# A depthwise convolution as block-Toeplitz matmuls: from 4 phases and 32 channels per block to 8 phases and 16 channels

## The reference, cut to what matters

```python
proj = h @ w_in                                   # (B, T, 5*D)
a, bg, u_pool, gate_a, gate_b = split(proj)
glu = a * sigmoid(bg)
conv, new_conv = causal_depthwise_conv(glu, conv_prev, conv_w, conv_b)   # width 31, per channel
y_a = silu(layer_norm(conv, conv_ln_g, conv_ln_b)) @ w_conv_out
pooled, new_pool = multiscale_pool(u_pool, pool_prev, pos0)  # trailing means over 2, 4, 8, 16
y_b = (einsum(pooled, pool_w) * pool_scale) @ w_pool_out
merged = sigmoid(gate_a) * y_a + sigmoid(gate_b) * y_b
return merged @ w_out, new_conv, new_pool
```

## Time and profile before

| | |
|---|---|
| median of 3 runs | 1577.0 us (1576.28 to 1577.05) |
| the profiled execution | 1571.29 us, span 1569.7 us (core 5, the slowest) |
| spans of the 8 cores | 1556.7 to 1569.7 us |
| busy, share of the span | PE 94%, PEld 55%, DVE 44%, ACT 30%, POOL 9% |
| mixer of A: GLU stage, pool and convolution stage | 545 to 605 us, 605 to 676 us |
| mixer of B: GLU stage, pool and convolution stage | 818 to 878 us, 878 to 946 us |

### The profile page before, as it was taken

The page is one execution under the profiler, slowest core; times in us unless marked ns, Lnnn a source line. Parts: engine busy times, 40 slices in busy tenths (PEclk is TensorE's granted clock), DMA queues, the critical chain, the costliest instruction groups (busy, mean ns, idle before and its releaser), DMA issues.

```text
span 1569.7 us, 24460 instructions; the slowest of 8 cores (1556.7 to 1569.7 us)
## 1 busy us (share of the span) xinstructions
PE 1479.4 (94%) x9258; PEld 856.3 (55%) x9258; DVE 688.6 (44%) x935; ACT 472.9 (30%) x688; POOL 133.9 (9%) x253
## 2 busy tenths in 40 slices
PE   0799999999899999999999999999999999999995
PEld 0466666544344457765664564445666665444454
DVE  1223323565222465972377687237431134441255
ACT  0011112253112264672127456113531111421124
POOL 2011111000110000000000000000000010000000
PEclk9999999999999999999999999999999999999998
DMA  9989999869977868635386964457586465584522
GB/s 185 180 141 196 196 215 186 167 110 190 186 137 145 144 155 232 182 72 131 55 174 143 243 182 105 97 104 154 118 178 131 74 132 97 111 170 84 113 70 99
DMA packets 94980, 227.03 MB, mean 145 GB/s; under 512 B 10848, under 2 KB 36192, under 8 KB 94688
## 3 DMA queue, kind: packets, MB, share of 16 engines
q0 software_dynamic: 37136, 124.11, 48.6%
q1 hardware_dynamic: 57728, 101.36, 20.9%
HBM read 299.64 MB, written 40.11 MB: 216 GB/s over the span
## 4 chain that ended last, share of the span: by engine, by line
PE 84%; DMA 9%; DVE 3%; ACT 2%; issue 2%; SPq 0%; DVEq 0%; ACTq 0%; POOL 0%; POOLq 0%
PE ps L354 78%; PE ps L769 4%; DMA VS<-pool_w 3%; DMA ring<-ffn_w_in 2%; DMA VS<-R 2%; DMA XS<-tp_dr 1%; DMA ring<-w_ada 1%; DVE VB L322 1%; PE ps L418 1%; DVE hA L319 1%; ACT L315 1%; ACT scr L315 0%; PE ps L544 0%; ACT rstd_sb L315 0%; ACT VB L315 0%
## 5 line engine op out<-in xcount | busy, mean ns | idle before, releaser
L354 PE MATMUL ps<-hA,ring 128*128 128x348 bf16 x3072 | 467.2, 312 | 8.1 <-DMA ring<-ffn_w_in 3.6
L354 PE MATMUL ps<-hB,ring 128*128 128x512 bf16 x2048 | 450.9, 380 | 10.0 <-DVE mpv L513 5.3
L354 PE MATMUL ps<-R,ring 128*128 128x348 bf16 (+3 forms) x2378 | 398.7, 327 | 0.0
L354 PEld LDWEIGHTS ps<-hA,ring 128*128 128x128 bf16 x3072 | 298.1, 97 | 170.1 <-issue 9.6
L354 PEld LDWEIGHTS ps<-hB,ring 128*128 128x128 bf16 x2048 | 200.0, 98 | 250.6 <-issue 15.7
L315 ACT ACTIVATE scr<-ps 128x1044 f32<-128x1044 f32 (+1 forms) x136 | 140.3, 1032 | 633.8 <-PE ps L354 629.8
L354 PEld LDWEIGHTS ps<-R,ring 128*128 128x128 bf16 x2378 | 229.3, 97 | 163.1 <-issue 0.2
L319 DVE TENSOR_TENSOR R<-ps,scr 128x1024 bf16<-128x1024 f32 (+2 forms) x112 | 128.8, 1156 | 429.9 <-PE ps L354 387.0
L315 ACT ACTIVATE scr<-VB 128x1044 f32<-128x1044 f32 (+3 forms) x56 | 51.5, 919 | 296.8 <-DVE VB L322 121.1
L322 DVE SCALAR_TENSOR_TENSOR VB<-ps,modT,XS 128x1024 f32<-128x1024 f32 (+4 forms) x56 | 55.1, 983 | 97.1 <-PE ps L354 94.1
L303 POOL DMA_DIRECT2D ring<-ffn_w_in x88 | 46.6, 531 | 470.8 <-PE ps L354 440.2
(11 more groups left out here) (121 smaller groups left out, 802.7 us busy)
## 6 DMA issues: line engine op xcount, KB each, us to landing
ring<-ffn_w_in POOLq DMA_DIRECT2D x88, 512.0 KB, 10.0
ring<-w_in POOLq DMA_DIRECT2D x40, 512.0 KB, 7.5
ring<-w_ada POOLq DMA_DIRECT2D x36, 512.0 KB, 15.8
ring<-ffn_w_out POOLq DMA_DIRECT2D x48, 352.0 KB, 6.3
XS<-tp_dr SPq DMA_DIRECT2D x48, 288.0 KB, 4.5
tp_dr<-VS SPq DMA_DIRECT2D x32, 288.0 KB, 15.5
XS<-x_b SPq DMA_DIRECT2D x16, 512.0 KB, 9.8
VS<-R SPq DMA_DIRECT2D x128, 64.0 KB, 5.6
```

The lines of the kernel that those rows point to most:

```text
L354: ins = e.matmul(o, lt, rt[:, c0:c0 + n], start=(i == 0), stop=(i == nk - 1))
```

## The change

It goes to NQ = 8 phases of NM = 128 columns: token 8m+q stands at phase q. A block now holds 16 channels by 8 phases, so 64 groups (NG) instead of 32, and ND = 5 shifts instead of 9. A group is 5 matmuls of 128 columns and has 160 KB of Toeplitz weights.

- Convolution: 640 matmuls of 128 columns for both mixers, instead of 576 of 256. A conv_unit still has 512 columns: 4 groups, each a recorded operation of its own with its own wait. 12 Toeplitz slots of 640 columns (nine in XS, three in poolw); two groups lie in one row of tp_dr.
- ACT: per unit 4 Identity of 128 columns and one Square of 512 that reads conv from SBUF, instead of 2 and 2 of 256 from PSUM. Silu: 4 of 128 per unit instead of 2 of 256.
- glu_move and the copies after Silu: 8 copies of 16 channels in runs of 128 bf16 (256 bytes) per chunk, instead of 4 with runs of 512 bytes.
- Pooling: halos of 4 columns instead of 6; the sum for windows of 8 is now two DVE instructions. In A the copies into U take several phases at once: 7 pieces instead of 6.
- conv_stats: 4 matmuls of 256 columns instead of 2 of 512; mean and rstd have 128 columns instead of 256.
- build_toep: 32 products of 1280 columns instead of 1152, in 6 slots instead of 7; cwv lies in hB and is 640 KB instead of 288 KB.

```diff
-NQ = 4
-NM = 256
-NG = 32
-ND = 9
-GHAL = 8
-UH = 6
+NQ = 8
+NM = 128
+NG = 64
+ND = 5
+GHAL = 4
+UH = 4
 UR = UH + NM
-NTOEP = 7
+NTOEP = 12
+TW = ND * 128
...
             def glu_move(c):
                 st = glst[:, c % 2, :]
-                pairs = [(GP[:, 4 * c + i, GHAL:], st[32 * i:32 * i + 32, :].rearrange("c (q m) -> c q m", q=NQ)) for i in range(4)]
+                n = 128 // NQ
+                pairs = [(GP[:, NQ * c + i, GHAL:], st[n * i:n * i + n, :].rearrange("c (q m) -> c q m", q=NQ)) for i in range(NQ)]
...
-                if c < NTOEP:
-                    tload(c)
+                for t in range(12 * c // 8, 12 * (c + 1) // 8):
+                    tload(t)
...
+            UG = 512 // NM
+
             def conv_unit(u):
                 bk = 6 + u % 2
-
-                def cmm(e):
-                    ins = None
-                    for t in range(2):
-                        gi = 2 * u + t
+                for t in range(UG):
+                    gi = UG * u + t
+
+                    def cmm(e, gi=gi, t=t):
+                        ins = None
                         for d in range(ND):
...
-                    act(sq[:, t * NM:(t + 1) * NM], ps[:, bk, t * NM:(t + 1) * NM], AF.Square, bias=cpv[:, 0, gi:gi + 1])
+                cu = lambda w: conv[:, UG * w:UG * w + UG, :].rearrange("p t n -> p (t n)")
+                act(sq, cu(u), AF.Square)
...
-                        tt(P[:, :, 4:UR], Q[:, :, 4:UR], Q[:, :, 3:UR - 1], ALU.add)
+                        wsum(P, Q, 3, 4)
...
-                            dma("sp", "sw%d" % (c % 4), [(d_[32 * i:32 * i + 32, :].rearrange("c (q m) -> c q m", q=NQ), s_[:, i, :]) for i in range(4)], [s_], [d_])
+                            dma("sp", "sw%d" % (c % 4), [(d_[nch * i:nch * i + nch, :].rearrange("c (q m) -> c q m", q=NQ), s_[:, i, :])
+                                                         for i in range(NQ)], [s_], [d_])
```

More of the change, by code:

```diff
@@ L843, in mixer @@
                     conv_unit(2 * i - 1)
-            conv_unit(NG // 2 - 2)
-            conv_unit(NG // 2 - 1)
+            conv_unit(NG // UG - 2)
+            conv_unit(NG // UG - 1)
             if first:
```

164 lines of the change are left out of this document (88 added, 76 removed).

## The result

The changed kernel takes 1603.05 us (median of 4 runs, 1597.63 to 1612.12) where the kernel before took 1577.03 beside it: ratio 1.0166, 95% interval 1.0112 to 1.0220. It is 26 us slower. I had forecast 1573.4 and a range up to 1590. In a second state, which every kernel falls into at times, the cores of a die show a lower granted clock and the time is longer; the times and ratios of this text are those of the other, faster state.

The account below looks back on a forecast made before the run. The kernel was taken as bound by TensorE, with DVE a few us behind in the pool and convolution stage; -16.1 + 4 + 5 + 3.5 = -3.6, from 1577.0 to 1573.4 us, range 1562 to 1590.

Parts of the forecast that it names:

- The convolution's matmuls: Convolution stage: 640 matmuls of 128 columns at 56 ns each, so PE gives back 27.2 us, 13.6 per mixer.
- Rival 3: Convolution: weight loads aren't hidden under 128 columns; 1582 us at 100 ns a matmul, 1588 at 109; chance 0.05.
- What ends the stage: Pool and convolution stage: DVE's last sum ends it in PE's place, 7.5 us earlier in A, 8.6 in B.
- -16.1: Pool and convolution stage: total forecast gain in us over both mixers, conv_stats coming 7.5 earlier in A, 8.6 in B.
- GLU stage: Eight copies per chunk instead of four: late issue on SP, mostly hidden, costs 1 us in A, 3 in B, +4.
- Gate B stage: SP's 64 copies at 0.61 us delay PE: +5 us in A through so2, +3.5 in B through the slst slot.
- The small packets: Copies in GLU and gate B stages: cost goes by bytes, a 256-byte packet about 14 ns, engines' work unchanged.
- Rival 2: Copies, mainly glu_move: small packets cost by number; 1580 us at 27 ns a packet, 1594 at 54; chance 0.30.
- Silu: Gate B stage, ACT: a Silu of 128 columns takes 0.385 us, a unit 1.54 us instead of 0.98.
- the signs that I had set for being wrong: SP not bounding the 64 copies, a crowded GLU stage stretching over 6 us, or DVE idle while PE awaits Toeplitz.
- The third: Sign of being wrong, convolution stage: DVE has idle time while PE waits for a Toeplitz block; no size given.
- Rival 4: Gate B stage: Silu and its copies cost more, ACT's slst waits pile up, +8 and +5.4, 1579 us; chance 0.05.

Follow-up runs that it names:

- e5: Changed kernel, with the second half's two weight blocks of the stage behind the convolution loaded only after the last convolution unit's square: 1584.6 us, ratio 1.0106.
- e6: e5, with the copies behind Silu split between SP and POOL and the second weight blocks recorded ahead of them on POOL: 1569.1 us, ratio 0.9998.
- e8: Changed kernel with only the first 12 Toeplitz blocks of each mixer loaded and DVE's running sums of units 2 to 14 left out: 1573.3 us, ratio 1.0012.
- e9: Changed kernel with four staging slots instead of two for the GLU stage's chunks: 1601.2 us, ratio 1.0155.
- e12: e6 plus GLU copies on two queues, that stage's second-half and the pooling projection's weight blocks issued earlier, and e9's four staging slots: 1569.7 us, ratio 0.9992.
- e14: e12, with the gate stage's first-half two weight blocks loaded in mid convolution stage, behind unit 5's square: 1567.3 us, ratio 0.9957.
- e1: Changed kernel with four of the eight copies behind Silu left out per chunk: 1580.1 us, ratio 1.0061.
- e4: Kernel before, with each copy behind Silu and in glu_move split in two by channels, 64 packets of 512 bytes each: 1593.5 us, ratio 1.0138.
- e10: e6, with the running sums of the squares in units 1 to 14 added on GpSimd instead of VectorE: 1588.7 us, ratio 1.0082.

## Why the prediction was wrong

**The convolution's matmuls: right.** 56 ns as taken. The Trainium skill's 81 ns (TensorE: Matmul & The Clock Gate, Back-to-back issue gap) does not hold for these pairs: the trace has 40 in 2.24 us. Rival 3 is out.

**What ends the stage: the mechanism right, its cover wrong.** DVE takes PE's place as the second limit. With the weights out of the way (e5, e6) the stage is 8.9 and 7.0 us shorter than before, where I said 7.5 and 8.6. The step that failed is "the few us of lead that PE has over DVE cover their landing; without it each collision with a weight load is a wait of 1 to 3 us". There is such a collision in each mixer; it costs 5.1 and 5.7 us (changed kernel less e5). The lead was there (4.25 us in e5), and the landing of 11 to 12 us is longer. I priced single waits of 1 to 3 us and left out three things: several blocks in a row are late, PE's granted clock falls behind the idle, to 0.76 as the mean of 21 us, and conv_stats stands behind 7.1 us of PE's own work, which the waits push out. Of -16.1 there remained -5.1. PE's own end in A, at 46.5 us after the first convolution group, was put 3 us too early as well (e8).

**GLU stage: mis-sized.** Forecast +4, measured +8.9. I saw SP's queue fill to 6.2 us of 7.1 per chunk, and still let most of the lateness hide in PE's slack. SP's timeline in A has eight copies in 5.1 to 9.9 us, and with the Toeplitz loads and the writes behind them several chunks take longer than the 7.1 at hand. e9 and e12 show that the slot was only where this was felt: with more slots the stage shrinks, and the late copies and blocks wait at the head of the next. Of what the two stages lose together, a part is the gate stage's first weight loads (e14 is 3.5 and 1.7 us under e12). How much of the rest is SP's issue, how much the landing and how much the smaller packets stays open.

**Gate B stage: the place right, the size half.** Forecast +8.5, measured +20.1, of which the number of copies makes 17 to 18 (e1, e4). "64 copies at 0.61 are 39.0 us" was 44.0, so the last landed by 57 us after conv_stats and not by 51 to 53. The larger error is the way to PE. In A I followed so2 at the very end; PE was hit 16 us earlier, by sbf, which stands behind the products on DVE, these behind tanh, and tanh behind a Silu that waits for a slot. In B the chain was the right one (slot, Silu, tanh, gate_mm), but I put it at the slot of chunk 3, for chunk 7, when the weight loads have passed. It was at the slot of chunk 1, for chunk 5: its copies had gone out by about 985 and Silu waited for them until 995.3, beside the same loads as in A. The wait was 9.1 us, not 3.5. And each idle brought slower matmuls behind it, 1.5 to 2.2 us. In the convolution and the gate stage, then, the same term was sized too small: a small transfer that someone waits for lands late beside a weight load. In the gate stage it is felt since the issues are late; the kernel before had the same landing of 8.4 us, and nothing waited for it.

**The small packets: near enough, and the rival that named them mostly wrong.** A packet of 256 bytes took 20 ns and not 14; the line through two mean sizes, 457 and 1774 bytes, each from a stretch with its own traffic, was a weak base. But e4, with packets of 512 bytes and the same number of copies, loses 17 of the 20 us of the gate stage and 6 of the 9 of the GLU stage. The rule of the Trainium skill (DMA: Bandwidth & Descriptors, Specifications) that transfers below 512 bytes leave line rate agrees with the trace in part: 20 ns for 256 bytes, 27 for 457. The packets took a quarter of the engines' time in the gate stage; by e4, some 3 us in each of the two stages are left that they may have cost. Rival 2 ended on the right side for the wrong reason.

**Silu: right.** 0.39 us, 16 in 6.25.

**Of the signs that I had set for being wrong**, SP was the bound of the copies, and no GLU stage stretched by over 6 us. The third came: in B, PE waited 6.8 us for three Toeplitz blocks near the head of the stage (904 to 914), and DVE stood idle for 5.1 us in three waits for what PE had not yet computed. The wait of PE for DVE before conv_stats, 5 to 10 us by the prediction, is not there in the changed kernel; e5 has 4.25. The forecast's own range, 1567 to 1579, took each term near its own estimate; three terms off to the same side by 5 to 12 us were not in it. Rival 4, Silu and its copies at +8 and +5.4, was the nearest: its place was right, and it had 5%. (By its own terms its time is 1578.3, not 1579.)

## What to carry to other kernels

A layout that halves the work of a matmul and doubles the number of small DMA issues can move the bound to the issuing queue, as here in the gate stage: count the issues per stage at the rate of a busy stretch, and compare it with the rate of the engine that produces them, chunk by chunk, not only at the end. The Trainium skill (DMA: Bandwidth & Descriptors, Issuing engines are not separate DMA queues) says that a second issuing engine saves only the issue, "usually small relative to the DMA itself"; here an issue of 0.69 us stands beside a landing of 2.1, 64 of them follow each other, and leaving out half of them was worth 18 of 20 us (e1). When a queue falls behind, ask for every instruction behind the waiting one on the next three engines. A load just in time, like the Toeplitz blocks, is only as good as its landing beside the largest weight load of the stage; where that is 11 us instead of 4.5, try to move the weight load, and look where the collision goes (e14). And before a remedy's gain is put down to a new layout, give the old one the same remedy.

## What the runs showed of the hardware that I had not expected

- SP's issue of a copy with a three-dimensional pattern costs the same with 128 packets of 256 bytes (44.01 us for 64) and with 64 packets of 512 bytes (43.85 for 64).
- 160-KB loads on SP's queue land in 4.5 us in the median of the span (of the changed kernel), and in medians of 7.8 to 13.1 beside three or four 512-KB loads of another queue (the changed kernel and e12).
- After 10.9 us without work PE's next 24 matmuls took 5.18 us instead of 3.71. After a wait of 4.3 us the granted clock was 0.50 for the next 8.4 us, and five matmuls took 0.69 us instead of 0.44: an idle costs more than its length.
- An add of 512 fp32 columns takes GpSimd 1.55 us where VectorE takes 0.69, and VectorE's 1024-column instructions beside it take 1.69 us instead of 1.23. A 16-column one went from 0.17 to 1.25 us and ended with GpSimd's add (e10).
